# A projection's last column block made four times wider and moved ahead of the third block, in a three-layer kernel with TensorE as its busiest engine

## What is computed

```python
h = rmsnorm(x, norm1_g[i])
p = h @ w_in[i]                # 1024 -> 2624 columns (some of them padding here): q, k, v, gates of three attentions
x = x + mixer(p) @ w_out[i]    # compressed/sliding, indexer-selected and dilated attention, 16 heads of 64
h = rmsnorm(x, norm2_g[i])
x = x + conv_glu_ffn(h, w_up[i], conv_w[i], conv_b[i], w_down[i])
```

## Time and profile before

| | |
|---|---|
| median of 3 executions | 1034.18 us (1031.78 to 1034.72) |
| the profiled execution | 1031.68 us |
| its span, first to last instruction | 1030.4 us |
| TensorE busy | 1018.5 us |
| VectorE, ScalarE, GpSimd busy | 765.7, 551.2, 225.9 us |
| mean granted TensorE clock | 0.999 |
| the two stretches that the change touches | about 33 to 124 us and 345 to 436 us |

### The profile page before, as it was taken

The page is one execution under the profiler, slowest core; times in us unless marked ns, Lnnn a source line. Parts: engine busy times, 40 slices in busy tenths (PEclk is TensorE's granted clock), DMA queues, the critical chain, the costliest instruction groups (busy, mean ns, idle before and its releaser), DMA issues.

```text
span 1030.4 us, 14765 instructions
## 1 busy us (share of the span) xinstructions
PE 1018.5 (99%) x5714; PEld 854.7 (83%) x5714; DVE 765.7 (74%) x1214; ACT 551.2 (54%) x831; POOL 225.9 (22%) x311
## 2 busy tenths in 40 slices
PE   9999999999999999999999999999999999999997
PEld 6877788888888877788888888997788878888886
DVE  6987678788777887578787778988855457666665
ACT  6475656555456466656554556656434545434432
POOL 0270600000000280600000003118967620000000
PEclk9999999999999999999999999999999999999999
DMA  9451445555554351365554554453445556555541
GB/s 360 150 203 47 146 182 183 189 188 202 195 188 169 118 215 42 123 216 194 209 201 167 205 177 161 154 203 105 165 145 197 210 183 223 180 206 189 179 149 41
DMA packets 26823, 179.16 MB, mean 174 GB/s; under 512 B 2945, under 2 KB 3073, under 8 KB 6273
## 3 DMA queue, kind: packets, MB, share of 16 engines
q1 hardware_dynamic: 26752, 178.22, 48.5%
HBM read 177.16 MB, written 1.05 MB: 173 GB/s over the span
## 4 chain that ended last, share of the span: by engine, by line
PE 92%; POOL 5%; issue 1%; DVE 1%; ACT 1%; DVEq 0%; POOLq 0%; ACTq 0%
PE pb L697 17%; PE pb L702 10%; PE pb L577 8%; PE pb L578 7%; PE pb L580 7%; PE pb L720 6%; PE pb L722 6%; PE pb L721 6%; POOL wlo L2605 5%; PE pb L703 2%; PE pb L958 2%; PE pb L914 2%; PE pb L926 1%; PE pb L659 1%; PE pb L622 1%; PE pb L624 1%
## 5 line engine op out<-in xcount | busy, mean ns | idle before, releaser
L1760 DVE TENSOR_TENSOR wlo<-raw,whi 128x2048 fp32r<-128x2048 f32 x127 | 290.6, 2290 | 108.1 <-ACT whi L1304 107.8
L1304 ACT ACTIVATE whi<-raw 128x2048 fp32r<-128x2048 f32 (+1 forms) x164 | 305.0, 1864 | 62.2 <-PE pb L580 32.9
L2605 POOL TENSOR_TENSOR wlo<-raw,whi 128x256 fp32r<-128x256 f32 x260 | 199.0, 803 | 320.6 <-ACT whi L1304 320.6
L697 PE MATMUL pb<-hb,whi 128*128 128x512 f32 x770 | 194.0, 391 | 0.0
L697 PEld LDWEIGHTS pb<-hb,whi 128*128 128x128 f32 x770 | 144.9, 188 | 28.8
L577 PE MATMUL pb<-whi,hb 128*128 128x512 f32 x344 | 137.5, 400 | 2.0 <-POOL wlo L2605 1.2
L578 PE MATMUL pb<-wlo,hb 128*128 128x512 f32 x344 | 134.0, 390 | 0.0
L580 PE MATMUL pb<-whi,hb 128*128 128x512 f32 x328 | 128.0, 390 | 0.0
L702 PEld LDWEIGHTS pb<-hb,wlo 128*128 128x128 f32 x880 | 120.0, 190 | 8.6
L702 PE MATMUL pb<-hb,wlo 128*128 128x256 f32 x880 | 122.7, 282 | 0.0
L720 PE MATMUL pb<-whi,gh 128*128 128x512 f32 x280 | 109.3, 391 | 0.0
(11 more groups left out here) (389 smaller groups left out, 1552.8 us busy)
## 6 DMA issues: line engine op xcount, KB each, us to landing
raw<-wst SPq DMA_DIRECT2D x160, 1024.0 KB, 4.8
raw<-wst SPq DMA_DIRECT2D x8, 512.0 KB, 3.9
gb<-gains SPq DMA_DIRECT2D x3, 512.0 KB, 5.7
X<-x SPq DMA_DIRECT2D x2, 512.0 KB, 5.6
out<-X SPq DMA_DIRECT2D x4, 256.0 KB, 2.1
PQ<-prm SPq DMA_DIRECT2D x1, 909.0 KB, 4.6
raw<-wst SPq DMA_DIRECT2D x2, 256.0 KB, 7.0
prmt<-prm SPq DMA_DIRECT2D x1, 479.0 KB, 9.8
```

Source lines behind the costliest of these rows:

```text
L697: e.matmul(both, wh[:, k, s], hb2[:, k, :, :].rearrange("p i q -> p (i q)"), start=k == 0, stop=False)
L1304: e.activation(whi[:, split_slot(m), 0:w], raw[:, m % RAW, 0:w], ACT.Copy).then_inc(*hi(m))
L1760: e.tensor_tensor(wlo[:, split_slot(m), 0:w], raw[:, m % RAW, 0:w], whi[:, split_slot(m), 0:w].bitcast(F32), ALU.subtract).then_inc(*lo_v(m))
L2605: g = e.tensor_tensor(wlo[:, split_slot(m), s], raw[:, m % RAW, s], whi[:, split_slot(m), s].bitcast(F32), ALU.subtract)
```

## The change

The last two blocks of the projection become 320 and 256 columns instead of 512 and 64; block 5 becomes one tile of eight times 256 columns. It stands in the stream directly behind block 4's and the compression's tiles, so ahead of blocks 2 and 3. It is computed as the others are, 128 tokens stationary, into the two halves of bank 7, at the head of `attention`, and ACT evicts it with two activations there. The copy, the two transposes and DVE's eviction go. The `ahead` calls that stood at `in 3` move by one place. `on_pool` is not touched.

```diff
-BLOCKS = [(0, 512), (512, 512), (1024, 512), (1536, 512), (2048, 512), (2560, 64)]
+BLOCKS = [(0, 512), (512, 512), (1024, 512), (1536, 512), (2048, 320), (2368, 256)]
...
-            plan += [("t", l, "in", b, 0, CH), ("t", l, "in", b, 1, CH)]
+            plan += [("t", l, "in", b, k, 4 * BLOCKS[b][1]) for k in range(2)]
             if b == 4:
-                plan += [("raw", l, "c", 0, 0, CH), ("raw", l, "c", 1, 0, CH)]
-        plan.append(("t", l, "in", 5, 0, 512))
+                plan += [("raw", l, "c", 0, 0, CH), ("raw", l, "c", 1, 0, CH), ("t", l, "in", 5, 0, 8 * BLOCKS[5][1])]
...
                 def last_values():
                     m = tile_at[l, "in", 5, 0]
...
                     bank_free(7)
-                    o = PB[7][0:64, 0:256]
-                    for k in range(8):
-                        q.wait_ge(*n1[k])
-                        e.matmul(o, wh[:, k, :], hh[:, k, :], start=k == 0, stop=False)
-                        e.matmul(o, wh[:, k, :], hl[:, k, :], start=False, stop=False)
-                        mm = e.matmul(o, wl[:, k, :], hh[:, k, :], start=False, stop=k == 7)
+                    for t in range(2):
+                        s, o = slice(128 * t, 128 * t + 128), PB[7][:, 256 * t:256 * t + 256]
+                        for k in range(8):
+                            q.wait_ge(*n1[k])
+                            e.matmul(o, hh[:, k, s], wh[:, k, :], start=k == 0, stop=False)
+                            e.matmul(o, hh[:, k, s], wl[:, k, :], start=False, stop=False)
+                            mm = e.matmul(o, hl[:, k, s], wh[:, k, :], start=False, stop=k == 7)
                     mm.then_inc(*used(m))
-                def last_values_turned():
...
+                    free[7] = proj(l, 5, 1)
...
+                last_values()
                 part(2, 0, 0)
                 part(2, 0, 1)
                 hidden_turned()
...
                 evicted(4)
+                evicted(5)
...
                 free[4], free[5] = mix_hl[l, 0], mix_hl[l, 1]
-                last_values()
                 scores(8)
-                last_values_turned()
                 out_half(0, 0, 0)
...
                 project(4, 0, 0)
                 transposed(7)
+                ahead(l, "in", 5, 0)
+                c0, w = BLOCKS[5]
+                q.wait_ge(*used[tile_at[l, "in", 5, 0]])
+                for t in range(2):
+                    e.activation(P[:, t, c0:c0 + w], PB[7][:, w * t:w * t + w], ACT.Copy,
+                                 scale=norm_of["n1", l][:, 6 + t:7 + t]).then_inc(*proj0(l, 5, t))
                 attention(l, transposed, project)
...
                 weights(2)
-                ahead(l, "in", 3, 0)
                 divided(2)
...
                 weights(6)
-                ahead(l, "in", 3, 1)
+                ahead(l, "in", 3, 0)
                 turned(5)
                 weights(7)
                 mixed(0)
                 mixed(1)
                 turned(6)
-                q.wait_ge(*used[tile_at[l, "in", 5, 0]])
-                q.wait_ge(*scored[l, 0, 3])
-                e.activation(rl[0:64, 0, 0:256], PB[7][0:64, 0:256], ACT.Copy).then_inc(*last_v(l))
-                ahead(l, "in", 5, 0)
+                ahead(l, "in", 3, 1)
                 weights(8)
...
                 highest(8)
-                c0, w = BLOCKS[5]
-                q.wait_ge(*mm_last[l])
-                for t in range(2):
-                    v = e.tensor_scalar(P[:, t, c0:c0 + w], PB[7][:, 256 + 64 * t:320 + 64 * t],
-                                        norm_of[n1][:, 6 + t:7 + t], None, ALU.mult)
-                v.then_inc(*dve(l, "last values"))
                 shares()
```

More of the change, by code:

```diff
@@ L320, in signals @@
             return [Signal(owner, sem(n)) for n in names.split()]
-        (warm_mm, half_used, used, turned, mm_qk, mm_idx, mm_cmp, mm_kv, mm_cs, mm_score, mm_pt, mm_val, mm_last, mm_ce,
+        (warm_mm, half_used, used, turned, mm_qk, mm_idx, mm_cmp, mm_kv, mm_cs, mm_score, mm_pt, mm_val, mm_ce,
          mm_small, mm_level, spread) = pe_all = signals(
-            TQ, "warm_mm half_used used turned mm_qk mm_idx mm_cmp mm_kv mm_cs mm_score mm_pt mm_val mm_last mm_ce "
+            TQ, "warm_mm half_used used turned mm_qk mm_idx mm_cmp mm_kv mm_cs mm_score mm_pt mm_val mm_ce "
                 "mm_small mm_level spread")
-        (hi, squares, diag, hh_done, proj0, qk_a, gate_exp, relu, tanh_h, exped, pt_a, last_v, ce_turned, mix_hh, act,
+        (hi, squares, diag, hh_done, proj0, qk_a, gate_exp, relu, tanh_h, exped, pt_a, ce_turned, mix_hh, act,
          ff_low, ff_cc, ff_tanh, gh_done, gated, normed_a) = act_all = signals(
-            SQ, "hi squares diag hh_done proj0 qk_a gate_exp relu tanh_h exped pt_a last_v ce_turned mix_hh act "
+            SQ, "hi squares diag hh_done proj0 qk_a gate_exp relu tanh_h exped pt_a ce_turned mix_hh act "
                 "ff_low ff_cc ff_tanh gh_done gated normed_a")
@@ L372, in proj @@
         def proj(l, b, t):
-            if t and b not in (2, 3):
+            if t and b not in (2, 3, 5):
                 return proj1[l, b]
@@ L378, in parts @@
         def parts(m):
-            return whi[:, split_slot(m), :], wlo[:, split_slot(m), :]
+            w = plan[m][5]
+            return whi[:, split_slot(m), 0:w], wlo[:, split_slot(m), 0:w]
         def two_on(*tile):
@@ L566, in tokens_half @@
                 wh, wl = (w.rearrange("p (k c) -> p k c", k=4) for w in parts(m))
-                s, o = slice(t * 128, t * 128 + 128), PB[bank][:, :]
+                s, o = slice(t * 128, t * 128 + 128), PB[bank][:, 0:wh.shape[2]]
                 weights_ready(m)
@@ L998, in last_values @@
                     m = tile_at[l, "in", 5, 0]
-                    wh, wl = (w[:, 0:512].rearrange("p (k c) -> p k c", k=8) for w in parts(m))
+                    wh, wl = (w.rearrange("p (k c) -> p k c", k=8) for w in parts(m))
                     weights_ready(m)
                     bank_free(7)
-                    o = PB[7][0:64, 0:256]
-                    for k in range(8):
-                        q.wait_ge(*n1[k])
-                        e.matmul(o, wh[:, k, :], hh[:, k, :], start=k == 0, stop=False)
-                        e.matmul(o, wh[:, k, :], hl[:, k, :], start=False, stop=False)
-                        mm = e.matmul(o, wl[:, k, :], hh[:, k, :], start=False, stop=k == 7)
-                    mm.then_inc(*used(m))
-                def last_values_turned():
-                    q.wait_ge(*last_v[l])
-                    for t in range(2):
[L1013 to L1016, removed]
+                    for t in range(2):
[5 more added lines that the diff above has]
+                            mm = e.matmul(o, hl[:, k, s], wh[:, k, :], start=False, stop=k == 7)
+                    mm.then_inc(*used(m))
+                    free[7] = proj(l, 5, 1)
                 def out_half(n, k, t):
```

8 lines of the change are left out of this document (4 added, 4 removed).

## The result

The changed kernel takes 1045.96 us, the median of five executions (1043.87 to 1046.79). The kernel before took 1031.78 (1031.27 to 1034.72) in the same comparison. The ratio is 1.0129 (1.0115 to 1.0142): slower by 14.2 us. The forecast had the sign and the place, but 8.1 us of cost, and its time of 1042.3 came out as near as it did partly because it was made on the higher median of 1034.18. The time lies 0.5 us above the top of the range.

The account below looks back on a forecast made before the run. It took TensorE to bound the kernel (busy 1018.5 of 1030.4 us). Block 2's delays, 4.8 + 4.6, less refunds of 2 x 0.65, gave +8.1 on the median 1034.18: 1042.3 us, 8-in-10 range 1037.5 to 1045.5.

Parts of the forecast that it names:

- TensorE's work: Matmuls of blocks 4 and 5: narrower widths and dropped transposes give 0.9 us less work a layer.
- When block 2 can begin: Block 2 waits for GpSimd's low part after block 5: 4.8 us late in the first layer, 4.6 in the second.
- its idle 0.89: Second layer, VectorE's idle wait for transpose 4: gained back because TensorE comes 1.9 us sooner.
- the 0.5: Second layer, an indexer step on VectorE now overlapping GpSimd's split: gives back 0.5 us of VectorE's gain.
- Where `last_values` stood: In front of `scores(8)`: removing 2.8 us of work refunds only 0.65 us a layer, since TensorE waits for ScalarE's exponentials.
- Behind block 2 all moves with TensorE: After block 2's start: other engines' work stays in time and keeps its distances, at no further cost.
- rival 4: Downstream of block 2: a further wait of 1 to 3 us a layer, VectorE slowed beside GpSimd's splits; chance 0.07.
- the sum: Both layers' block 2 delays less two refunds: 4.8 + 4.6 - 2 x 0.65 = +8.1 us.
- Rival 3, the clock: Waits around block 5 lower the granted clock, block 2 some 4 us later again, 1051 us in all; chance 0.04.

Follow-up runs that it names:

- run 12: Changed kernel, block 5 back at its old place, block 2's first low part on VectorE, GpSimd held until VectorE's gelu is done: 1032.57 us, ratio 1.0006.
- run 6: Changed kernel with the old widths of 512 and 64 columns, block 5 still computed ahead of block 2: 1047.18 us, ratio 1.0146.
- run 1: Changed kernel with the low part of block 3's first tile made by VectorE instead of GpSimd: 1041.35 us, ratio 1.0089.
- run 9: Changed kernel with block 5's low part made by VectorE in front of the rotation, instead of GpSimd: 1042.94 us, ratio 1.0104.
- run 2: Changed kernel with ScalarE's split of block 2's first tile ahead of the indexer's third relu: 1042.42 us, ratio 1.01.
- run 3: Changed kernel with twelve matmuls of 512 columns, results unread, added in front of `scores(8)`: 1045.76 us, ratio 1.0137.
- run 4: Changed kernel with the new widths only, block 5 computed and evicted at its old place, last in the stream: 1032.13 us, ratio 1.0016.

## Why the prediction was right and where it was not

*TensorE's work: right.* 320 columns are 0.1467 us apart (34.72 to 37.95 in 22 steps), 256 columns 0.120, and run 12 shows 1.0 us less work a layer (forecast 0.9). The line through two points holds between 256 and 512 only. Run 6 shows that below it there is next to nothing to save: 0.111 at 64 columns. TensorE's busy time didn't fall by 2 us, though; it rose from 1018.5 to 1020.3. Some 1.6 of that is the stretch at the lower clock. From `indexer(1)` to the output projection it is 72.85 us instead of 72.68 in the first layer, where the spacings say 0.9 less; a matmul ahead of a wait counts with its whole length there, and how far that explains it was not followed up.

*When block 2 can begin: right.* Bank 7 was free at 47.2 (forecast 47.35), the wait for GpSimd 1.51 (1.55), block 2 at 54.72 (54.8). In the second layer it came 5.16 later, not 4.6. VectorE there, before and after:

```profile
351.10 0.29 DVE L1876 TENSOR_TENSOR sc<-sc,mskt 128x128 f32<-128x128 f32 x1
...
352.96 0.66 DVE L516 TENSOR_TENSOR sm<-PQ,prmt 128x128 f32<-128x128 f32 x1
```

```profile
359.27 0.80 DVE L1871 TENSOR_TENSOR sc<-sc,mskt 128x128 f32<-128x128 f32 x1
...
360.66 0.86 DVE L516 TENSOR_TENSOR sm<-PQ,prmt 128x128 f32<-128x128 f32 x1
...
365.14 0.27 DVE L1865 TENSOR_SCALAR sc<-rl,PQ 128x128 f32<-128x128 f32 x1
```

VectorE did lose its idle 0.89. But it comes to L1865 12.30 us behind the start of `indexer(1)` (352.84), before 12.29, so nothing of the 0.5 is left: the operations in front of the rotation now stand beside GpSimd, which starts at 359.18. The step to which the forecast gave the 0.5 took 0.27, as before; the loss is elsewhere on the same chain. In run 1 the second layer's block 2 comes 4.63 later, so this varies. What the forecast missed is why this chain is so long. It took the chain's end from the rows, and in it the six operations of the rotation at up to 0.83 us, beside GpSimd. Runs 6 and 9 show 0.28.

*Where `last_values` stood: right.* 0.56 and 0.54 us refunded, 0.65 forecast. Two waits on L908, 0.67 and 0.63, and one on L577, 0.61, stand where 1.7 and 0.5 us were foreseen.

*The failed step is "Behind block 2 all moves with TensorE".* It asked whether each engine is in time if everything keeps its durations. They don't: before, VectorE's scalings fell in a pause of GpSimd's pieces and the small operation beside them was let through; after, the small operation is held to the end of the 24 pieces, and the scalings miss the pause (65.64 to 67.85) and fall on the next eight. That is 2.2 us a layer, 4.4 in all, and run 1 takes 4.6 us off by closing that one contact. Run 2 closes it in another way, with the same waits gone. It was rival 4, which had 0.07, and at its middle size. The rival named the very row, 49.15 to 66 (48.96 to 65.64 measured), but the sum put it at nothing, because GpSimd's pieces were checked only for when they are needed, not for who runs beside them.

*Rival 3, the clock, was right in kind and wrong in place.* Nothing falls in the waits around block 5 (both layers at 1.00). It falls behind the waits at `scores(8)`, which the forecast had itself put at 1.7 us and more, by 1.5 us, in some executions, and the sum had no term for it; run 3 shows that it is the gap. The Trainium skill, "TensorE: Matmul & The Clock Gate", section "Why this matters for your kernels", warns against idle gaps between bursts. The trace agrees only in part: a gap of the size that it gives isn't here, no single wait is longer than 0.67, and three of them with little work between did it.

*The sum.* In the profiled executions: 4.70 + 5.16 for block 2, 2 x 2.2 behind it, 1.5 for the clock, -1.1 refunded. That makes 14.7, and the two spans differ by 14.4. Without its 1.5 the profiled execution would have taken 1044.6, and the two executions of the highest clock took 1043.87 and 1044.05; these last 0.6 us or so aren't settled. Why the small step is caught in one layer and not in the other of the same execution (run 4) was not tried, and stays open.

*Was the move worth repairing?* The best form of it is 1039.17 or 1039.19, still 8.3 and 7.3 us above the kernel before beside it. The best form of the widths alone equals before. Nothing here beats it.

## What to carry to other kernels

For a move, ask whether each engine is still in time, and also whether VectorE and GpSimd are pushed on top of each other. So look, for each operation of VectorE on the path, at what GpSimd does in that stretch before and will do after, and suspect a wait in a duration that is three times that of the same operation elsewhere. A lead that TensorE gains in front of a stretch bound by VectorE and ScalarE can be lost there (1.6 of 3.9 us in run 12), and work put behind the stretch is paid in full (3.0). And a block that is split into narrower matmuls costs by their number once they are narrow.

## What the runs showed of the hardware

- *VectorE can stand for several GpSimd instructions.* The operation on 32 columns took 0.18 us with GpSimd idle. Beside a row of GpSimd's pieces it took 0.31 and 0.66 (before, the two layers), 0.35 (run 2), 2.15 and 2.14 (after), 2.15 (run 9) and 3.63 (run 4); the last four ended with the row. What decides between the short and the long ones isn't known. In the other direction a VectorE operation of 2.28 us made eight pieces take 7.68 instead of 5.6.
- *Spacing of matmuls* in fp32r, on 128-wide weights, at full clock: 0.111 us at 64 columns, 0.120 at 256, 0.147 at 320, 0.227 at 512. From 256 down to 64 it hardly falls.
- *The granted clock fell with TensorE busy all the time.* In run 6 the engine shows 3.30 of 3.30 us busy with matmuls of 64 columns, and then the granted clock is 0.51, the lower level, and the same matmuls are 0.213 us apart, still without a wait. In the second layer it fell too (0.69 from 372 to 378). Being busy all the time didn't hold the clock here.
